# A merge stage whose modulation rows are fetched on the weights' queue, and whose branch product waits once

## The reference

```python
# first block, the merge
y_sb = jnp.einsum('bse,ed->bsd', o_sb, w_branch_sb[l])
y_gdn = jnp.einsum('bse,ed->bsd', o_gdn, w_branch_gdn[l])
merged = jax.nn.sigmoid(gate_sb) * y_sb + jax.nn.sigmoid(gate_gdn) * y_gdn
x = x + jnp.einsum('bsd,de->bse', merged, w_out[l])
# second block, the modulation: 6*1024 sums over 1024 products
cond = jax.nn.silu(c)
mod = cond @ ada_w[i] + ada_b[i]
```

## Time and profile before

| | us |
|---|---|
| three runs | 2715.97, 2718.2, 2719.17 (median 2718.2) |
| the profiled execution | 2715.97 |
| its span in the profile | 2714.2 |
| PE busy in the span | 2644.4 (97%) |
| the merge on PE | about 626 to 844 |
| DMA traffic | 501.14 MB, 185 GB/s on average |

### The profile page before, as it was taken

One profiled execution on the slowest core, in us unless ns is written; L12 is line 12 of the kernel. 1 busy time (PEld: TensorE's weight loads), 2 busy tenths in 40 slices (PEclk: granted clock), 3 DMA queues, 4 the chain that ended last, 5 costly groups with the idle time before them and its releaser, 6 DMA issues.

```text
span 2714.2 us, 36027 instructions
## 1 busy us (share of the span) xinstructions
PE 2644.4 (97%) x13669; PEld 2275.6 (84%) x13669; DVE 1848.1 (68%) x3465; ACT 1141.7 (42%) x1893; POOL 568.7 (21%) x463
## 2 busy tenths in 40 slices
PE   8999999999999999999999999999999999999998
PEld 6887888888888999999998888888888656788886
DVE  4456565756665687877996888888987495544433
ACT  6544454344224445455663333333332455423223
POOL 0111110111112878772001111111110033000001
PEclk9999999999999999999999999999999999999999
DMA  4111201005662678765779889989986211222230
GB/s 172 55 55 61 95 32 47 32 32 209 244 221 93 240 275 297 275 235 208 275 278 330 332 321 364 335 325 345 343 324 225 87 55 47 101 93 93 93 105 35
DMA packets 141500, 501.14 MB, mean 185 GB/s; under 512 B 13288, under 2 KB 66960, under 8 KB 111888
## 3 DMA queue, kind: packets, MB, share of 16 engines
q1 hardware_dynamic: 115984, 339.43, 34.6%
q0 software_dynamic: 25344, 159.39, 15.2%
HBM read 450.53 MB, written 48.25 MB: 184 GB/s over the span
## 4 chain that ended last, share of the span: by engine, by line
PE 85%; DVE 11%; ACT 2%; DMA 1%; POOL 1%; issue 1%; SPq 0%; ACTq 0%; DVEq 0%; POOLq 0%
PE bank L264 23%; PE bank L266 23%; PE bank L265 23%; DVE HA L2204 3%; PE bank L1174 2%; PE bank L1190 1%; DVE HO L2201 1%; PE bank L2720 1%; PE bank L789 1%; DVE uhl L1733 1%; PE bank L1180 1%; PE bank L2754 1%; PE bank L779 1%; PE bank L802 1%; PE bank L2827 1%
## 5 line engine op out<-in xcount | busy, mean ns | idle before, releaser
L264 PE MATMUL bank<-HH,uhl 128*128 128x384 f32 x1024 | 346.4, 338 | 4.4 <-POOL uhl L1733 4.4
L266 PE MATMUL bank<-HH,uhl 128*128 128x384 f32 x1024 | 343.7, 336 | 0.0
L265 PE MATMUL bank<-HL,uhl 128*128 128x384 f32 x1024 | 343.3, 335 | 0.0
L1789 POOL DMA_INDIRECT gs<-in_uv_dram,idx x128 | 153.2, 1197 | 751.5 <-DVE x L1814 486.7
L264 PE MATMUL bank<-vhl,awhl 128*128 128x512 f32 x768 | 300.2, 391 | 7.4 <-DVE awhl L2453 7.4
L266 PE MATMUL bank<-vhl,awhl 128*128 128x512 f32 x768 | 299.8, 390 | 0.0
L265 PE MATMUL bank<-vhl,awhl 128*128 128x512 f32 x768 | 299.8, 390 | 0.0
L2388 ACT ACTIVATE vhl<-vraw 128x1024 fp32r<-128x1024 f32 x128 | 135.8, 1061 | 315.9 <-PE bank L266 274.4
L264 PE MATMUL bank<-HH,whl 128*128 128x512 f32 x528 | 212.5, 403 | 1.2 <-DVE HL L396 1.2
L266 PE MATMUL bank<-HH,whl 128*128 128x512 f32 x528 | 206.0, 390 | 0.0
L265 PE MATMUL bank<-HL,whl 128*128 128x512 f32 x528 | 205.8, 390 | 0.0
(11 more groups left out here) (452 smaller groups left out, 6068.1 us busy)
## 6 DMA issues: line engine op xcount, KB each, us to landing
ur<-in_peer_u_dram SPq DMA_DIRECT2D x128, 512.0 KB, 5.3
vraw<-in_peer_v_dram SPq DMA_DIRECT2D x128, 512.0 KB, 6.5
w_raw<-in_w_in_dram SPq DMA_DIRECT2D x35, 1024.0 KB, 4.8
xn<-in_ada_rows_dram POOLq DMA_DIRECT2D x48, 512.0 KB, 5.8
g_scratch<-stg SPq DMA_DIRECT2D x12, 2048.0 KB, 8.8
gti<-g_scratch SPq DMA_DIRECT2D x16, 1536.0 KB, 11.8
wf_raw<-in_f_w_in_dram SPq DMA_DIRECT2D x22, 1024.0 KB, 4.8
act_scratch<-ag SPq DMA_DIRECT2D x96, 192.0 KB, 3.2
```

The lines of the kernel that those rows point to most:

```text
L264: e.matmul(out, l[0], r[0], start=start, stop=False)
L265: e.matmul(out, l[0], r[1], start=False, stop=False)
L266: return e.matmul(out, l[1], r[0], start=False, stop=stop)
L1789: e.indirect_dma_start(gs[:, n % 4, :], None, a["uv"], bass.IndirectOffsetOnAxis(ap=idx[:, n:n + 1], axis=0)).then_inc(*gs_land[n % 4].up(n))
```

## The change

Two edits. The PE's waits for the low blocks are gathered: each branch product now waits, before its first matmul, for the last of the eight low blocks (in stages 0 to 3 those of the attention's output, in 4 to 7 those of the GDN's). And the 48 fetches of `ada_rows` go from POOL's stream to SP's: three ahead of tile 30, then six behind each pair of weight fetches. They keep their waits for mod m-3.

```diff
     def pe_merge_branch(e, s):
         e.wait_ge(*W.low(k).of(k))
+        e.wait_ge(*V.of("low", s // 4, 7))
...
             for j in range(KT):
-                if f == 0 and s % 4 == 0:
-                    e.wait_ge(*V.of("low", s // 4, j))
...
-    def pool_mod(e, m):
+    def sp_mod(e, m):
         if m < 48:
             if m >= 3:
                 e.wait_ge(*MG[2].of("mod", m - 3))
...
     def pool_merge(e):
-        all_done(e, *GH)
-        for m in range(48):
-            pool_mod(e, m)
         split_lo(e, W, W_OUT1 + 4)
...
         e.dma_start(cond, a["c_b"]).then_inc(*cond_land.up("c"))
+        for m in range(3):
+            sp_mod(e, m)
         for s in range(8):
             fetch(e, W, 30 + 2 * s)
             fetch(e, W, 31 + 2 * s)
+            for m in range(6 * s + 3, 6 * s + 9):
+                sp_mod(e, m)
         for k in range(46, 49):
             fetch(e, W, k)
```

## The result

The changed kernel takes 2740.7 us (median of six runs, 2738.29 to 2742.05) against 2718.66 us of before (six runs): a ratio of 1.0078 with a 95% interval of 1.0068 to 1.0088, or 22 us slower. The sign was forecast, the size was not: 2726 was forecast, and 2740.7 lies outside 2719 to 2738.

What follows compares the result with a forecast made beforehand. PE, busy for 97% of the span, was taken as the bound. Waits of 1.9 + 1.2 + 3 x 0.7 + 1.2 + 2.4 = 8.8 us on the 2718.2 median gave 2727.0; forecast 2726, range 2719 to 2738.

Steps and rivals of the forecast that it cites:

- PE's waits at the places named: PE gaps at the first branch product, gates of stages 5 and 6, branch of 7, and two in the output product.
- the gathered wait's 1.9 us: First branch product: PE waits from 637.38 until DVE's eighth low block at 639.24, 1.9 us on the path.
- the last wait's 2.4 us: Output product's third row block: PE waits 2.4 us for PSUM banks that DVE frees with stage 7's products.
- D + 6.3: Even weight tiles land 6.3 us after D, the end of a stage's last mod, behind three mod fetches in order.
- s = 0 to 2: D = A + 7.6, hidden, with 3.6 us to spare: Stages 0 to 2: tile usable 18.15 us after A, PE's branch product end; wanted at 21.76, so no wait.
- forecast to cost 1.2 us on its own: Stage 3, where eight low blocks come between: PE waits 1.2 us ahead of the gate product of stage 5.
- my 22.45: Stages 4 to 6: one loop turn takes 22.45 us against PE's 21.76, costing 0.7 us in each of three turns.
- is covered at stage 4 by 1.9 us: Stage 4: low blocks end at 722.77, PE needs them at 724.7, so gathering their waits costs nothing there.
- The clock rival: PE's granted clock falls after the new waits in the merge, adding 1.6 to 5 us: 2728 to 2732; chance 0.06.
- Shared tiles: Both weight tiles of a pair share the DMA engines, landing at D + 7 to 8.8: 2730 to 2742; chance 0.14.
- The queue is hidden: Weights on SP land within 5.4 us of D, only the gathered wait costs: 2720 to 2723.5; chance 0.26.
- The bound of D + 8.8: High end of the weight tile's landing, sharing engines evenly with the next tile; some 24 us in all.

Runs made afterwards that it cites:

- The burst: Against the kernel with only the mod fetches moved to SP: each stage's last three mod fetches wait together, then issue back to back ahead of the weights; 2744.82 us.
- the kernel with the other order: Against the kernel with only the mod fetches moved to SP: weight and mod fetches issued in the order in which DVE releases them; 2720.55 us.

## Why the prediction failed

**What held.** The mechanism: weights behind a mod fetch that waits for DVE, a loop through SP, the DMA, ACT and DVE, slower than PE's 21.76 us; PE's waits at the places named; the gathered wait's 1.9 us (2.2); the last wait's 2.4 us (2.2), released by a product of line 1628; POOL's part free. The last wait holds beyond this one profile: from the start of the output product to the end of the merge it is 55.6 us here and 55.7 and 55.9 in the other two profiles of the change, against 53.3 before. How this shows on PE differs: in the other two the wait ahead of the third row block is 0.6 us and none, the one at the start 3.9 and 4.3 us, and slow matmuls in between take up the rest. The merge is where the loss is, and everything behind it moved as a whole.

**The step that failed first: the landing, "D + 6.3".** It was 7.3 to 8.3, over the seven even tiles from 32 to 44. In stage 4 of the change the last mod, 29, ends DVE's stage at 759.1, the tile leaves at 759.53, and ACT begins its high part when it has landed:

```profile
759.05 0.08 DVE L1600 DVE_READ_ACCUMULATOR xn<-xn,eg 128x1 f32 x1
```
```profile
756.87 2.62 SPq L1607 DMA_DIRECT2D xn<-in_ada_rows_dram  x3
759.53 0.43 SPq L234 DMA_DIRECT2D w_raw<-in_w_in_dram  x1
```
```profile
766.90 1.92 ACT L241 ACTIVATE whl<-w_raw 128x2048 fp32r<-128x2048 f32 x1 [6.01 <-DMA w_raw<-in_w_in_dram]
```

The three mods issued from 756.87 on, one each 1.15 us, took these times to land, the tile behind them the last:

```profile
xn<-in_ada_rows_dram SPq DMA_DIRECT2D x1, 512.0 KB, 3.3
...
xn<-in_ada_rows_dram SPq DMA_DIRECT2D x1, 512.0 KB, 4.3
...
xn<-in_ada_rows_dram SPq DMA_DIRECT2D x1, 512.0 KB, 5.3
...
w_raw<-in_w_in_dram SPq DMA_DIRECT2D x1, 1024.0 KB, 7.3
```

Landings at 760.2, 762.3, 764.5 and 766.8: in order, as I had it, but a mod held the queue for 2.15 us, not for the 1.25 that I took from the difference of two undisturbed landings. Two of them make 1.8 us more, less 0.4 elsewhere. The burst shows that the 1.25 was right for a full queue; why fetches that come 1.15 us apart go at about half the rate (238 to 262 GB/s in the same situation in the variant with the weights further ahead, where the DMA engines' busy share was 1.02 from 750 to 752 all the same) was not tried further and stays open.

**The step that failed second: "s = 0 to 2: D = A + 7.6, hidden, with 3.6 us to spare".** I let the loop close only where PE first waits. It closes as soon as the tile is later than DVE's other work, which needs no waiting PE. Tile 32 was usable at 674.6, and PE began with it at 676.16, so of the 3.6 us to spare 1.5 were there. ACT's high part of it waits for the DMA in stage 1 already:

```profile
670.48 1.92 ACT L241 ACTIVATE whl<-w_raw 128x2048 fp32r<-128x2048 f32 x1 [4.40 <-DMA w_raw<-in_w_in_dram]
...
693.35 1.92 ACT L241 ACTIVATE whl<-w_raw 128x2048 fp32r<-128x2048 f32 x1 [5.51 <-DMA w_raw<-in_w_in_dram]
...
716.20 1.92 ACT L241 ACTIVATE whl<-w_raw 128x2048 fp32r<-128x2048 f32 x1 [6.60 <-DMA w_raw<-in_w_in_dram]
...
743.17 1.91 ACT L241 ACTIVATE whl<-w_raw 128x2048 fp32r<-128x2048 f32 x1 [10.87 <-DMA w_raw<-in_w_in_dram]
```

The turns are 22.9, 22.9, 27.0 (with the low blocks) and then 23.7, 24.1 and 23.3. The first two are 2.2 us over PE's pace together: they eat the 1.5 us unseen and cost the first 0.9, at the gate of stage 4. The third, forecast to cost 1.2 us on its own, costs 4.3 at the gate of stage 5. The last three are 0.8 to 1.7 us longer than my 22.45, by the landing.

**The third: the gathered wait "is covered at stage 4 by 1.9 us".** The cover was DVE's promptness, which the other edit takes away: 0.8 us. Alone, the gathered wait is covered there.

**The clock rival** named the right event and the wrong price. The clock falls to half behind gaps (0.50 above), but inside a loop that sets the pace the slow matmuls only fill waiting time. Where no wait for the loop follows at once, as behind the first gap with the gathered wait alone, a dip costs 1.6 us, as reckoned from the earlier trace rows.

**The rivals on the fetches.** *Shared tiles* had the size (2730 to 2742) but not the cause: the two tiles of a pair land 2.5 to 3.6 us apart, in order. *The queue is hidden* did not come true for the change; it is what the kernel with the other order shows. The Trainium skill ("DMA: Bandwidth & Descriptors", section "Issuing engines are not separate DMA queues") says that spreading DMAs over several issuers saves only the sequencer's time to start them; that kernel agrees, with all mods through SP and 223.78 us for the merge. What the rule leaves out is a waiting fetch, with its bytes, ahead of the weights: that is the 16.3 us. The Trainium skill ("DMA: Bandwidth & Descriptors", section "Queues, rings and completion order") has each DMA engine take the descriptors of one ring in order; the landings above (760.2, 762.3, 764.5 and 766.8) agree with it.

The range failed with the landing. I had written that it counts four times; it counts for all seven tiles, with 1.0 to 2.0 us each, and what the slack of the first ones does not take makes up most of the 8.8 us that the forecast lacks in the merge. The bound of D + 8.8 was in the text, and I gave it too little room. The merge's 17.7 to 20.0 us on top of 2718.66 would be 2736.4 to 2738.7, at the edge of the range; beyond it the 2740.7 stand also by the 2 to 4 us outside the merge that no run places.

## What to carry to other kernels

A fetch that waits for a late consumer holds back everything issued behind it: put the issues of one queue in the order in which their waits are released. Here the queue could then be shared for nothing. When a transfer is made to wait for the engine that will later need its data, write the whole turn of that loop down and hold it against the pace of the bounding engine from the first turn on, since slack is used up turn by turn before any wait shows. Slow matmuls cost nothing where PE has to wait for such a loop right behind them, and a wait costs next to nothing while the turn stays under the pace (1.0 us here); shortening the loop by one place in the stream gave back nearly half of the loss.

## What was not expected of the hardware

- A 512 KB fetch behind another one held SP's queue for 2.15 us when they were issued 1.15 us apart, and for 1.25 us when issued 0.4 us apart; a 1 MB tile right behind the last of them took 2.3 to 2.4 us in either case. The cause is open.
- A gap of 2.1 us on PE brought eight matmuls 0.43 us apart in two of four profiles with the same gap, and none in the others; the gap of 4.3 to 5.6 us ahead of the gate of stage 5 did in all five profiles that leave it unfilled.
